# Layer 1 of a two-layer diffusion block: which heads are asked for one tile and which for all four at the start of the expert stage

## The chip, the cores and the metric

The kernel runs on one NeuronCore of a Trainium2 chip, in float32. The metric is the device time of one execution in microseconds (us): the median of three runs of the kernel before is 4263.29 us, with runs from 4258.36 to 4267.86 us.

## What is computed

Two consecutive layers of a diffusion backbone over 512 latent tokens and 256 context tokens of width 1024. Layer 0 mixes tokens with Fourier groups and a bidirectional state-space scan, layer 1 with latent attention. After each mixer comes the expert stage, which is all that matters here. It runs over blocks of 128 tokens, called tiles; layer 1 has four (the latent tokens only).

```python
def one(hb):                                   # one tile of 128 tokens
    q = (hb @ p["peer_wq"]).reshape(128, 8, 2, 128)
    s = jnp.einsum("thsd,hskd->thsk", q, p["peer_keys"])
    s_top, i_top = lax.top_k(s, 16)
    cand = (s_top[:, :, 0, :, None] + s_top[:, :, 1, None, :]).reshape(128, 8, 256)
    g_score, c_idx = lax.top_k(cand, 16)
    experts = e1 * 128 + e2                    # from i_top and c_idx
    gates = jax.nn.softmax(g_score, axis=-1)
    act = gelu(jnp.einsum("thkd,td->thk", peer_u[experts], hb)) * gates
    return jnp.einsum("thk,thkd->td", act, peer_v[experts])
```

For each token and each of 8 heads, two query halves are scored against 128 keys each, the best 16 of the 256 best sums are chosen, and the 16 experts' rows (1024 numbers of u and 1024 of v) are gathered from a table of 16384 experts.

## The kernel before, in words

`peer_block` (L1541) writes the expert stage of either layer; the table `PEER_MAPS` (L1502) holds what differs, and its second entry (L1520) is layer 1. Five engines run their own instruction streams and meet at semaphores; within a stream everything is in order.

**Asking.** An *event* is a head with the tiles it is asked for at once. Two query products, one for each half (`query`, L1974, its products on L1987), hold a 128x128 block of the head's query weights in the tensor engine (PE) and stream 128 columns for each tile of the event, over 8 blocks; then `scores` (L1991, products on L1998) multiplies by the keys, one product for each tile and half. ACT copies both out of the accumulation banks (`query_out` L2252, `scores_out` L2264). Before each event, SP loads its weights: two halves of 512 KB of the query weights (`load_side`, L1788) and 128 KB of keys (`load_keys`, L1792), one event ahead: the half of the next event is asked for when the product of this event's same half is done. Neighbouring events with the same head would share a load; `load_of` counts loads. Before, layer 1 has twelve events and twelve loads: heads 0 to 3 for tile 0, heads 4 to 7 for tiles 0 to 3, then heads 0 to 3 for tiles 1 to 3.

**Choosing.** The vector engine (DVE) picks the experts of one (head, tile), a *choice*, in two halves of work (`choose_a` L2524, `choose_b` L2555); a product on PE spreads it over the partitions (`spread_choice`, L1954, products on L1968), and `choice_out` (L2585, reading on L2590) writes the experts' numbers and gates. `order` lists the choices in the order in which they are made.

**Using.** A *step* is one (head, tile): 16 gathers of 1 MB each, one expert row for every token of the tile. Layer 1 has 32 steps in the order given by `heads`, four batches of four gathers each, 128 batches. POOL issues a gather (L1896) into one of 12 slots when its choice is written and the slot is free. DVE takes the dot products with the tokens (`dot_batch`, L2606, on L2614), ACT the gelu and the scaled diagonals (`diagonals`, L2432 and L2438), PE adds the weighted rows into two banks (L2186) and thereby frees the slots. The first 16 gathers use 8 slots; the other four are free once the attention's output product (`project`, L1914) is done.

**What sets the order.** All engines count batches. `half_at` (L1576) puts choice 2 into batches 3 and 4 and each later choice into the next two batches, so that the last of the 32 is made in batch 64. `query_at` (L1584 to L1588) then puts an event's first product five batches ahead of its first choice, at least two batches after the event before; its second product and first scores come one batch later, its second scores two. So before, events 4 to 11 start at batches 2, 6, 10, 14, 18, 24, 30 and 36. Events 0 to 3 and choices 0 and 1 are written out by hand in the opening, between the output products of the attention. In a batch, PE does the products of that batch first, then what is due of choices, spreads and events. `kept` names the events whose scores keep a buffer of their own; the others use two in turn. In batches 4 and 5, 36 and 37, and 68 and 69, PE also spreads the rows of the next tile (`spread_rows`, L1940).

The lines of SP's program that fix a load's place:

```python
sp.wait_ge(qmm["sem"], at(qmm, 2 * e - 1))
load_side(e, 0)
if e >= 2:
    sp.wait_ge(smm["sem"], at(smm, 2 * loads[n - 1]))
    load_keys(e)
sp.wait_ge(qmm["sem"], at(qmm, 2 * e))
load_side(e, 1)
```

Of the kernel before, what the change touches and what calls it, by code (L numbers as in the profile page):

```python
# [40 lines left out]
PH, PK, PQ, TOPK = 8, 128, 256, 16  # L41
# [1325 lines left out]
def attention_stage(core, d):  # L1367
# [30 lines left out]
    with nc.Block() as block:  # L1398
# [75 lines left out]
        def _(act):  # L1474
            for n in range(N + 2):
# [25 lines left out]
ALL = tuple(range(PH))  # L1501
# [15 lines left out]
     "rep": (L0 + 3072, L0 + 5120), "ht": HO,  # L1517
     "slots": [L0 + 7168 + n * ROWS for n in range(4)] + [RO + n * ROWS for n in range(6)] +
              [L0, L0 + 7168 + 4 * ROWS]},
    {"events": [(h, (0,)) for h in range(4)] + [(h, (0, 1, 2, 3)) for h in range(4, PH)] +  # L1520
               [(h, (1, 2, 3)) for h in range(4)],
     "heads": (ALL,) + (ALL[4:] + ALL[:4],) * 3, "kept": (4, 5, 6, 7),
     "order": [(h, 0) for h in range(4)] + [(h, t) for h in range(4, PH) for t in range(2)] +
              [(h, t) for h in range(4) for t in range(1, 4)] + [(h, t) for t in range(2, 4) for h in range(4, PH)],
     "choose_from": 3, "early": 2, "ahead": 4, "asked_from": 0, "spread_at": (4, 5), "spread_first": (4, 5),
     "halves": tuple((t, c) for t in range(TL) for c in range(2)),
     "opening": tuple(range(8)) * 2, "ready": 8, "column": (), "near": 2, "halved": (),
# [1386 lines left out]
ALL = ("ada0", "mix0", "mix1", "peer1")  # L2914
# [82 lines left out]
```

## Time and profile before

| | |
|---|---|
| median of three runs | 4263.29 us (4258.36 to 4267.86) |
| the profiled execution's own time | 4261.36 us |
| its span, first to last instruction | 4259.6 us |
| mean granted TensorE clock | 0.853 of full speed |
| PE busy | 3048.2 us (72%) |
| DVE busy | 2863.2 us (67%) |
| ACT busy | 1195.6 us (28%) |
| POOL busy | 1564.9 us (37%) |
| moved from memory | 1473.31 MB, of which 1342.26 MB by gathers |

The two expert stages take the larger part of the span: layer 0 has 768 gathers, layer 1 has 512, the first of them issued at 2921.8 us and the last at 4232.6 us. A line of the page gives an engine's busy time and its share of the span; a tenths line cuts the span into 40 slices of 106.5 us, each digit the busy share; the transfer line is the mean over the core's 16 DMA engines, and under it stand the GB/s that they moved. A line of the timeline starts with the start and the length in us (several instructions in a row are merged, and their number stands at the end), and in brackets stands how long the engine had been idle before it and what ended that. Large products of float32 appear as two records each.

### The profile page before, as it was taken

The numbers are of one execution on the slowest core, as the hardware profiler recorded it, in microseconds if no ns is written. First come the engines' busy times: TensorE is split into PE (matmuls) and PEld (weight loads), VectorE is DVE, ScalarE is ACT, GpSimd is POOL, SyncE is SP. The second block draws the span as 40 slices with busy tenths as digits, with TensorE's granted clock in tenths as the row PEclk, the third lists the DMA queues.
The fourth block names the chain that finished last, engine by engine and source line by source line (L and its number), as shares of the span: only waits on it lengthen the run. The fifth ranks groups of instructions, "written<-read, shape, count | busy, mean of one in ns | idle before, by whom it ended". The sixth has DMA issues, their size and how long they took to land. (4 is left out here: it accounts for less than half of the span.)

```text
span 4259.6 us, 37648 instructions
## 1 busy us (share of the span) xinstructions
PE 3048.2 (72%) x11946; PEld 1284.5 (30%) x11946; DVE 2863.2 (67%) x7196; ACT 1195.6 (28%) x3222; POOL 1564.9 (37%) x1352
## 2 busy tenths in 40 slices
PE   8999899766767755555666677998876654555556
PEld 4655444322222212111222223664322211111111
DVE  2436846998888897555555665665888898555555
ACT  2125423323223222111222353563332322111111
POOL 0002213454544454444444441002444555444443
PEclk9999999888788877777788888999987877777777
DMA  4114859999999999999999997106999999999998
GB/s 178 41 39 180 301 200 360 408 421 416 421 420 393 421 421 418 422 422 414 420 418 419 417 416 272 40 1 248 412 420 420 419 421 414 421 421 418 419 421 357
DMA packets 234010, 1481.23 MB, mean 348 GB/s; under 512 B 26060, under 2 KB 37548, under 8 KB 63572
## 3 DMA queue, kind: packets, MB, share of 16 engines
q0 software_dynamic: 184320, 1342.26, 76.2%
q1 hardware_dynamic: 48116, 132.61, 8.5%
q10 hardware_dynamic: 1376, 3.96, 0.2%
q8 instruction: 95, 1.56, 0.1%
q14 instruction: 103, 0.84, 0.1%
HBM read 1473.31 MB, written 5.42 MB: 347 GB/s over the span
## 5 line engine op out<-in xcount | busy, mean ns | idle before, releaser
L2186 PE MATMUL banks<-arena 128*64 128x512 f32 x5104 | 1636.3, 801 | 1152.8 <-ACT arena L2438 1094.9
L1896 POOL DMA_INDIRECT arena<-experts,arena x1280 | 1505.0, 1176 | 2221.3 <-PE banks L2186 1542.7
L2614 DVE CUSTOM_DVE_ANT_0 arena<-arena 128x1024 f32<-128x1024 f32 x1280 | 1538.9, 1223 | 841.5 <-DMA arena<-experts,arena 841.0
L2186 PEld LDWEIGHTS banks<-arena 128*64 128x64 f32 x5104 | 450.3, 182 | 2256.8 <-ACT arena L2438 1268.3
L2432 ACT ACTIVATE arena<-arena 128x4 f32<-128x4 f32 x319 | 65.9, 206 | 2267.7 <-DVE arena L2614 2267.6
L2438 ACT ACTIVATE arena<-arena 128x64 f32<-128x64 f32 x1276 | 339.3, 336 | 37.7 <-ACT arena L2432 1.2
L1987 PE MATMUL banks<-arena 128*128 128x512 f32 (+3 forms) x960 | 288.9, 455 | 6.7 <-DMA arena<-wq 5.6
L453 PE MATMUL banks<-arena 128*128 128x512 f32 (+1 forms) x640 | 210.3, 489 | 1.9 <-ACT arena L514 1.9
L1987 PEld LDWEIGHTS banks<-arena 128*128 128x128 f32 x960 | 160.5, 191 | 115.6 <-issue 90.2
L1914 PE MATMUL banks<-arena 128*128 128x512 f32 x416 | 187.9, 601 | 7.3 <-DMA arena<-l_w_out 3.1
L453 PEld LDWEIGHTS banks<-arena 128*128 128x128 f32 x640 | 121.3, 191 | 87.2 <-issue 78.6
L2432 ACT ACT_TABLE_LOAD x109 | 139.8, 1283 | 1.9
L942 POOL TENSOR_TENSOR arena<-arena 128x192 f32<-128x192 f32 x1 | 0.6, 579 | 305.1 <-POOLq L398 305.1
L2602 DVE TENSOR_TENSOR arena<-arena 128x512 f32<-128x512 f32 x160 | 109.7, 686 | 0.2 <-DVE arena L2592 0.2
L1914 PEld LDWEIGHTS banks<-arena 128*128 128x128 f32 x416 | 77.0, 191 | 97.6 <-issue 90.2
L2614 DVE DVE_READ_ACCUMULATOR2_ANT arena<- 128x1 f32 x1280 | 104.0, 81 | 0.0
L2279 ACT ACT_TABLE_LOAD x80 | 102.6, 1283 | 1.4
L1448 DVE TENSOR_REDUCE arena<-banks 128x1 f32<-128x768 f32 x64 | 61.1, 955 | 57.8 <-PE banks L1411 56.4
L1411 PE MATMUL banks<-arena 96*128 96x512 f32 (+1 forms) x256 | 94.7, 493 | 2.4 <-PEq L1785 1.5
L474 PE MATMUL banks<-arena 128*128 128x512 f32 x192 | 83.2, 593 | 0.0
L1482 ACT ACTIVATE arena<-banks 128x768 f32<-128x768 f32 x64 | 51.9, 810 | 67.9 <-PE banks L1420 67.9
L582 DVE TENSOR_SCALAR arena<-arena 128x772 f32<-128x772 f32 x16 | 10.9, 681 | 87.9 <-ACT arena L524 87.9
(269 smaller groups left out, 3039.0 us busy)
## 6 DMA issues: line engine op xcount, KB each, us to landing
arena<-l_w_ada SPq DMA_DIRECT2D x48, 1024.0 KB, 8.3
arena<-wq SPq DMA_DIRECT2D x54, 512.0 KB, 8.0
arena<-experts,arena POOLq DMA_INDIRECT x1280, 17.5
arena<-l_w_in SPq DMA_DIRECT2D x6, 2048.0 KB, 7.8
arena<-l_w_out SPq DMA_DIRECT2D x4, 1536.0 KB, 14.4
arena<-l_w_o SPq DMA_DIRECT2D x4, 1024.0 KB, 8.4
arena<-keys SPq DMA_DIRECT2D x27, 128.0 KB, 10.8
arena<-gates SPq DMA_DIRECT2D x6, 512.0 KB, 12.2
```

The source lines that it names most:

```text
L453: i = pe.matmul(o[:, a:b], wt[:, k, (u % 4) * P:(u % 4 + 1) * P], ht[:, k, a:b], start=(k == 0), stop=(k == KD - 1))
L474: i = pe.matmul(core["ps"][:, n % 4, :], ht[:, k, t * P:(t + 1) * P], wt[:, k, :], start=(k == 0), stop=(k == KD - 1))
L1411: i = pe.matmul(o[:, a:b], qt[0:QK, h, q * P:(q + 1) * P], kt[0:QK, h, a:b], start=True, stop=True)
L1896: pool.indirect_dma_start(slots[n], None, tbl, bass.IndirectOffsetOnAxis(ap=expert[:, ring[c], k:k + 1], axis=0)).then_inc(land[n]["sem"], ...
L1914: i = pe.matmul(core["ps"][:, bank_of(t, c), :], lhs(k, t), wcols[c][:, k, :], start=(k == 0), stop=(k == K - 1))
L1987: i = pe.matmul(out, wq[:, side, k, :], ht[:, g[0]:g[-1] + 1, k, :], start=(k == 0), stop=(k == KD - 1))
L2186: mm = pe.matmul(core["ps"][QS * j:QS * j + QS, c, :], diag[:, g % 2, k, :], v[:, D + c * 512:D + (c + 1) * 512], start=(g % (NB * PH) == ...
L2279: act.activation(raised, shifted, ACT.Exp, accum_out=total[:, 0:1]).then_inc(exd["sem"], up(exd))
L2432: act.activation(gel[:, s], dots[:, s], ACT.Gelu).then_inc(gl["sem"], up(gl))
L2438: ins = act.activation(diag[:, g % 2, j, :], gated[:, b // 2, b % 2 * BATCH + j, :], ACT.Copy, scale=gel[:, b * BATCH + j:b * BATCH + j + 1])
L2602: dve.tensor_tensor(gated[:, n % 2], ident2.unsqueeze(1).to_broadcast([P, TOPK // 2, QS]), bcast(gate[:, ring[c], n % 2 * 8:n % 2 * 8 + 8] ...
L2614: dve.tensor_tensor_reduce(u, u, rep[i // PH % 2][:, k % NQ, :], 1.0, 0.0, ALU.mult, ALU.add, dots[:, k:k + 1]).then_inc(dot["sem"], up(dot))
```

## The change

Only layer 1's entry of `PEER_MAPS` is edited. Heads 0 to 6 are asked for tile 0 alone, head 7 for all four tiles, and heads 0 to 6 follow for tiles 1 to 3. That makes fifteen events and fifteen loads. Only head 7's event keeps a buffer of its own. The steps of tiles 1 to 3 begin with head 7, and the choices are made in an order to match. The planner then starts events 4 to 14 at batches 2, 4, 6, 8, 12, 18, 24, 30, 36, 42 and 48.

```diff
-    {"events": [(h, (0,)) for h in range(4)] + [(h, (0, 1, 2, 3)) for h in range(4, PH)] +
-               [(h, (1, 2, 3)) for h in range(4)],
-     "heads": (ALL,) + (ALL[4:] + ALL[:4],) * 3, "kept": (4, 5, 6, 7),
-     "order": [(h, 0) for h in range(4)] + [(h, t) for h in range(4, PH) for t in range(2)] +
-              [(h, t) for h in range(4) for t in range(1, 4)] + [(h, t) for t in range(2, 4) for h in range(4, PH)],
+    {"events": [(h, (0,)) for h in range(7)] + [(7, (0, 1, 2, 3))] + [(h, (1, 2, 3)) for h in range(7)],
+     "heads": (ALL,) + (ALL[7:] + ALL[:7],) * 3, "kept": (7,),
+     "order": [(h, 0) for h in range(PH)] + [(7, 1)] + [(h, t) for h in range(7) for t in range(1, 4)] +
+              [(7, t) for t in range(2, 4)],
```

## Rows read from the trace of the kernel before

**Rows 1.** The page, busy time of each engine, and transfers over 40 slices.
```profile
PE 3048.2 (72%) x11946; PEld 1284.5 (30%) x11946; DVE 2863.2 (67%) x7196; ACT 1195.6 (28%) x3222; POOL 1564.9 (37%) x1352
...
DMA  4114859999999999999999997106999999999998
GB/s 178 41 39 180 301 200 360 408 421 416 421 420 393 421 421 418 422 422 414 420 418 419 417 416 272 40 1 248 412 420 420 419 421 414 421 421 418 419 421 357
```

**Rows 2.** Windows of layer 1's expert stage; columns are in the first line.
```profile
core 0: us, PE busy (x) PEld busy (x) DVE busy (x) ACT busy (x) POOL busy (x), PEclk, DMA share, GB/s
...
2970.00:2980.00 10.00, 8.55 (x60) 5.86 (x56) 5.89 (x14) 5.29 (x12) 7.86 (x8) 1.00 0.93 340
2980.00:2995.00 15.00, 9.73 (x22) 4.03 (x24) 13.48 (x45) 3.58 (x10) 0.81 (x1) 0.77 1.01 417
2995.00:3015.00 20.00, 20.00 (x115) 9.56 (x113) 11.36 (x39) 7.68 (x17) 7.85 (x9) 1.00 0.99 381
3015.00:3300.00 285.00, 211.12 (x830) 85.98 (x828) 250.53 (x741) 86.75 (x215) 138.85 (x108) 0.84 1.01 420
...
3360.00:3380.00 20.00, 12.00 (x59) 4.95 (x59) 18.32 (x55) 7.20 (x17) 10.50 (x9) 0.85 1.00 405
...
3520.00:3600.00 80.00, 42.22 (x160) 12.98 (x160) 72.03 (x215) 20.78 (x53) 40.92 (x32) 0.78 1.00 411
3600.00:4200.00 600.00, 341.07 (x1030) 95.60 (x1032) 320.08 (x525) 80.87 (x306) 256.33 (x237) 0.75 1.01 420
```

**Rows 3.** Waits of DVE, 2980 to 3060, then 3060 to 3600: total, times, longest.
```profile
DVE arena L2590 <- PE banks L1968: 6.7, 2, 6.0
...
DVE arena L2614 <- DMA arena<-experts,arena: 16.7, 17, 2.1
```

**Rows 4.** Transfers, 3050 to 3300: rate, queues, issues with median landing.
```profile
DMA packets 15776, 104.95 MB, mean 420 GB/s; under 512 B 1746, under 2 KB 2386, under 8 KB 3718
...
q0 software_dynamic: 13551, 98.68, 95.0%
q1 hardware_dynamic: 2212, 6.11, 6.3%
...
arena<-wq SPq DMA_DIRECT2D x10, 512.0 KB, 8.0
arena<-experts,arena POOLq DMA_INDIRECT x95, 17.4
arena<-keys SPq DMA_DIRECT2D x5, 128.0 KB, 10.7
```

**Rows 5.** Transfers, 3700 to 3900.
```profile
DMA packets 11559, 84.18 MB, mean 421 GB/s; under 512 B 1287, under 2 KB 1287, under 8 KB 1287
...
arena<-experts,arena POOLq DMA_INDIRECT x81, 17.5
```

**Rows 6.** Timeline of PE around batches 3 and 4, and one three-tile query side.
```profile
2975.02 3.74 PE L1987 MATMUL banks<-arena 128*128 128x128 f32 x32
...
2985.27 8.55 PE L1987 MATMUL banks<-arena 128*128 128x512 f32 x16 [5.60 <-DMA arena<-wq]
2993.75 3.65 PE L2186 MATMUL banks<-arena 128*64 128x512 f32 x16
...
2998.33 7.03 PE L1987 MATMUL banks<-arena 128*128 128x512 f32 x16
3005.29 3.65 PE L2186 MATMUL banks<-arena 128*64 128x512 f32 x16
...
3215.14 5.43 PE L1987 MATMUL banks<-arena 128*128 128x384 f32 x16
```

**Rows 7.** Timeline of POOL: first gathers of batches 6 and 7.
```profile
2995.95 0.94 POOL L1896 DMA_INDIRECT arena<-experts,arena  x1 [15.14 <-PE banks L2186]
...
3007.49 0.94 POOL L1896 DMA_INDIRECT arena<-experts,arena  x1 [6.88 <-PE banks L2186]
```

**Rows 8.** Line 1789, the query weights, 2900 to 3320.
```profile
DMA to landing us min/median/max: 3.3/8.0/13.8
```

## Prediction

> **What bounds the kernel now.** I read the profile from coarse to fine. First the whole span [rows 1]: no engine is busy for three quarters of it, but the transfer line shows 9 in nearly every slice of the two expert stages, at 414 to 421 GB/s. Then the stretch that the change touches, layer 1's expert stage from about 2920 us to the end, cut by windows [rows 2]. The reader should look at the last two columns: from 2970 us to 4200 us the transfer engines are busy at 0.99 or more of their time, but for 0.93 in the first 10 us, and in the long windows they move 420 GB/s whether the tensor engine is busy 0.75 of the time (3015 to 3300) or 0.57 (3600 to 4200). So the bytes set the end of this stage, and the 512 gathers are nearly all of them. Only four rows stay below 415 GB/s: 340 in 2970 to 2980, 381 in 2995 to 3015, 405 in 3360 to 3380 and 411 in 3520 to 3600. Against 420 those are 10 x 80/420 = 1.9 us, 20 x 39/420 = 1.9 us, 20 x 15/420 = 0.7 us and 80 x 9/420 = 1.7 us of transfer time not used. That is all that any rearrangement can win in there, 6.2 us. Third, the vector engine, which stands close behind: it is busy 0.88 of 3015 to 3300 and 0.90 of 3520 to 3600 [rows 2], and in all of 3060 to 3600 it waited only 16.7 us for a gather to land [rows 3]. So there are two limits near each other in the first half of the stage, and the transfers are the nearer.
>
> **The change, part by part.**
>
> *Three more weight loads.* An event loads two 512 KB halves of the query weights and 128 KB of keys: 1152 KB, 1.18 MB. Twelve events become fifteen, so 3.54 MB more, nine more transfers on SP's queue. The price per byte comes from two stretches. In 3050 to 3300 five events' loads pass beside 95 gathers [rows 4]; in 3700 to 3900 there is no load and there are 81 gathers [rows 5]. The total rate is 420 against 421 GB/s, so a load does not ride free, it takes the place of gathers. By the rate, 3.54 MB / 0.420 = 8.4 us. By what the loads' own queue used, 6.3% of 250 us for 6.11 MB is 2.58 us per MB, or 9.1 us. I take 8.7 us, between the two ends. All three new transfers' groups fall between batch 2 and batch 43, inside the stretch that runs at 420, so nothing covers them. The Trainium skill, DMA: Bandwidth & Descriptors, section Anatomy of one DMA, gives another price: a fixed 2.0 us for each transfer beside bytes / 436 GB/s. Paid one after the other that would be an estimate of 9 x 2.0 + 8.1 = 26 us; the trace does not agree, since ten half loads and five key loads passed in [rows 4] with no drop of the rate.
>
> *Shorter queries in the opening.* Heads 4, 5 and 6 are asked at batches 2, 4 and 6 (before: 2, 6, 10) and for one tile; head 7 at 8 for four tiles; heads 0 to 6 follow at 12, 18, 24, 30, 36, 42, 48 for three (before: four such at 18 to 36). A query side takes 3.74 / 2 = 1.9 us at one tile, 5.4 at three, 7.0 at four, and 8.55 us for the first one of head 4 [rows 6]. Where it hurts now: that first one waits 5.6 us for its weights, starts at 2985.27, and batch 3's products stand behind it until 2993.75, then the second side holds batch 4's until 3005.29 [rows 6]. POOL's next gathers wait 15.1 and 6.9 us for exactly those products [rows 7], and the rate falls to 381 [rows 2]. After the change the same weights land at the same time, so the 5.6 us stay; the side then takes 1.9 us at full clock, up to 3.7 us at half of it. Batch 3 starts 8.55 - 3.7 = 4.9 to 6.6 us sooner, and batch 4, with 7.0 - 1.9 = 5.1 us more, 10 to 11.7 us sooner. That is more than the shortfall of 1.9 us, so I take all of it back: -1.9 us. The bounds are 0 (a new wait) and -3.8 us (the hole at 2970 to 2980 too). I leave that hole in, because it ends before the first changed query starts. The vector engine gains as well: its 6.0 us wait for the tensor engine's spread of choice 2 [rows 3] should go, which lets it lie behind the transfers instead of beside them.
>
> *The end of the choosing.* The choices keep their rate, one in two batches until batch 64, so their vector time is the same. The shortfall of 3520 to 3600 comes after the last loads (batch 31 before, batch 43 after), when the vector engine no longer keeps ahead of the gathers. With more bytes and a vector engine that is 6 us further on, it should shrink; between 0 and -1.7 us, I take -0.9. The shortfall at 3360 to 3380 stays: a three-tile query still meets the spread of tile 2's rows at batch 36.
>
> *At nothing.* The tensor engine's sum: 8 x 1.9 + 8 x 7.0 + 8 x 5.4 = 114 us of query sides before, 14 x 1.9 + 2 x 7.0 + 14 x 5.4 = 116 us after. Its 2 us lie in stretches where it is busy three quarters of the time; without that cover they would cost 2 us. Twelve more evictions on ACT, which is busy 0.30 of 3015 to 3300 [rows 2], stand behind work of the same batch. The keys' wait on SP has only loads behind it; the store of tile 0 now stands ahead of head 5's loads, and goes out when the tile is done, at batch 32, as before. Scores are made per tile, 64 products before and after. The choice for step 16 is now out in batch 61, at the last allowed place, but the gathers it feeds wait for batch 61's products anyhow, and those follow the dots after which it is written.
>
> **Sum.** 8.7 - 1.9 - 0.9 = +5.9 us. The profiled execution took 4261.4 us (its span of 4259.6 and 1.8 around it), 1.9 us under the median of 4263.3; it would become 4267.3, and the median 4269.2 us, +0.14%. About 0.2% (8.5 us) is what a measurement of this kernel can tell from no change, so this is called the same.
>
> **The rivals.**
>
> *Slower: the loads at full price and nothing back.* The new loads of heads 5, 6 and 7 come two batches apart, some 20 us, and crowd the transfers just where they were short of gathers; a query that waits for its weights, as the first one of head 4 does for 5.6 us [rows 6], holds a batch's products and then the gathers. It decides if a weight load takes longer to land than the two batches it is given. Then the price is 9.1 us, plus up to two holes of 1.9 us like those of now: 4272.4 to 4276.2 us. For it: the loads are asked in order on one queue, each only after the query before it. Against it: landing took 8.0 us in the median and 13.8 at most [rows 8], under 20. Part of this case is that only the shortfall is misjudged: at 8.7 us alone the median is 4272.0, just beyond 0.2%.
>
> *Faster or level: the vector engine is the real limit of the first half.* Then loads cost nothing while gathers wait for dots, and the waits of 6.0 us and 0.7 us for the tensor engine [rows 3] come straight off: 4263.3 - 6.7 = 4256.6 us. For it: only 16.7 us of waiting for gathers in 540 us [rows 3]. Against it: the transfers have no such 6.7 us to give; they ran at 1.01 of their time through 3015 to 3300 [rows 2], and 3.54 MB more must pass.
>
> *A fixed price per transfer.* If each transfer held the engines for a time of its own beside its bytes, nine more would cost more than 3.54 MB. The fastest half load landed 3.3 us after its issue [rows 8], and its 0.52 MB at 420 GB/s are 1.25 us of that; the other 2.05 us, nine times, and 8.4 us for the bytes make 26.9 us, or 4290.2 us. Against it: fifteen loads passed in [rows 4] with the rate of [rows 5]. The page's formula above is this case.
>
> That the edit does less than it says (a load saved where two neighbouring events share a head) is out: no two neighbours in the new list do.
>
> **How the numbers follow.** The sum 0.63; slower 0.27; the vector engine as limit 0.07; a fixed price 0.03. The range goes from 4261 (the sum with its low bounds, 8.4 - 3.8 - 1.7 = +2.9 or 4266.2, and 5 us below it, as the runs shown lie up to 5 us from their median) to 4277 (the slower rival's upper end). Slower by over 0.2%: most of the slower rival, the fixed price and a small upper part of the sum, 0.29. Faster by over 0.2%: half of the vector engine's case, 0.04. The rest, 0.67, lies within.
>
> **What would show it.** Right: 30 half loads and 15 key loads in the stage in place of 24 and 12; the rate in the 20 us after head 4's first query near 420; POOL's 15.1 us wait cut by 5 us or more; the vector engine's wait for gathers over the choosing half above 16.7 us, as the transfers are now plainly the limit; the stretch from there to batch 64 longer by 6 to 7 us, and nothing different after. Wrong: a rate below 400 GB/s in the opening, DMA as the releaser of several queries, or gathers released by the vector engine's choices. If the rate stays at 420 and the end comes no later, the loads were hidden, and the first reading of the bound was false.

## The result, and the profile after

The changed kernel takes 4266.6 us (median of 18 runs) and the kernel before, in 18 runs beside them, 4259.4 us. The ratio is 1.0017 with a 95% interval of 1.0010 to 1.0023: 7.2 us longer, between 4 and 10 us. Forecast were +5.9 us and a time within 0.2%. The medians of before lie 4 us lower here than in the three runs that the prediction had, so the ratio counts, not the absolute time.

The profiled execution after has a span of 4266.2 us against 4259.6, 6.6 us more; the readings below are of this one. Behind the table every line number is one lower than before, because the table is one line shorter.

First the transfers of the stage, 2900 to 4270: queues, then issues with their size and median landing.

```profile
q0 software_dynamic: 73728, 536.90, 94.6%
q1 hardware_dynamic: 6624, 18.48, 3.5%
...
arena<-wq SPq DMA_DIRECT2D x28, 512.0 KB, 8.1
...
arena<-keys SPq DMA_DIRECT2D x13, 128.0 KB, 11.4
```

With the two groups loaded before 2900 that makes 30 half loads and 15 key loads. The gathers' bytes did not change; SP's queue moved 18.48 MB where it had moved 14.94, which is 3.54 MB more.

Now the windows of [rows 2], after; the last two columns are the share of time in which the transfer engines were busy and the GB/s.

```profile
2970.00:2980.00 10.00, 8.36 (x59) 5.72 (x54) 5.90 (x13) 5.48 (x13) 7.87 (x8) 1.00 0.93 358
2980.00:2995.00 15.00, 9.56 (x52) 6.72 (x54) 13.47 (x45) 5.75 (x17) 3.86 (x4) 0.77 1.00 403
2995.00:3015.00 20.00, 15.63 (x142) 10.25 (x140) 18.20 (x54) 5.74 (x16) 9.78 (x9) 0.94 1.02 416
3015.00:3300.00 285.00, 197.74 (x776) 80.80 (x772) 242.48 (x721) 83.03 (x213) 134.66 (x104) 0.85 1.01 420
...
3360.00:3380.00 20.00, 13.81 (x58) 5.57 (x56) 15.81 (x49) 6.02 (x13) 10.12 (x10) 0.86 1.02 419
...
3520.00:3600.00 80.00, 41.49 (x160) 12.63 (x158) 72.03 (x216) 21.66 (x56) 41.01 (x32) 0.78 1.01 412
3600.00:4200.00 600.00, 343.26 (x1024) 95.88 (x1020) 323.41 (x536) 79.81 (x302) 261.40 (x240) 0.74 1.01 420
```

The hole of 381 GB/s at 2995 to 3015 is filled to 416; the one at 2970 to 2980 stays, 358 for 340; in 2980 to 2995 the rate is lower than it was, 403 for 417. The one at 3360 to 3380 is gone from that window, and the low rate at 3520 to 3600 is still there, 412 for 411. In the two long windows the rate is what it was, with more to carry.

The tensor engine (PE) around batches 3, 4 and 5 after, from the timeline, to be held against [rows 6]:

```profile
2985.44 3.58 PE L1986 MATMUL banks<-arena 128*128 128x128 f32 x16 [5.97 <-DMA arena<-wq]
2988.95 3.65 PE L2185 MATMUL banks<-arena 128*64 128x512 f32 x16
...
2992.85 1.95 PE L1986 MATMUL banks<-arena 128*128 128x128 f32 x16
2994.73 3.65 PE L2185 MATMUL banks<-arena 128*64 128x512 f32 x16
```

And POOL's first gathers of batches 6 and 7, against [rows 7]:

```profile
2991.15 1.36 POOL L1895 DMA_INDIRECT arena<-experts,arena  x1 [10.53 <-PE banks L2185]
...
2996.94 1.02 POOL L1895 DMA_INDIRECT arena<-experts,arena  x1 [0.69 <-PE banks L2185]
```

Head 4's first side still waits for its weights (5.97 us for 5.60), then takes 3.58 us, nearly twice the 1.95 us of its second side: the tensor engine had stood idle ahead of it, and its granted clock was 0.50 from 2982 to 2988, the lower of its two levels (1.2 of 2.4 GHz), before and after alike. Batch 3's products start 4.8 us sooner and batch 4's 10.6 us sooner, and the gathers of batches 6 and 7 go out 4.8 and 10.6 us sooner. Following the first gather of each batch further shows where that lead goes: batch 8 is 9.4 us ahead, batch 12 is 0.2 us behind, batch 24 1.3, batch 40 1.1, batch 48 7.3, batch 64 7.0 and batch 127 6.9 us behind. The lead of ten microseconds is gone within five batches: gathers asked for sooner stand longer in the queue. Those issued from 2990 to 3055 land 20.2 us after their issue in the median, where they took 10.8 before. The transfers had been short of work for less than 2 us there. From there the new loads add up until the last of them; from batch 48 on the lag stays between 5.8 and 7.8 us.

The vector engine's (DVE) waits after, 2980 to 3060 and then 3060 to 3600: total, times, longest.

```profile
DVE arena L2613 <- DMA arena<-experts,arena: 6.7, 6, 1.3
...
DVE arena L2613 <- DMA arena<-experts,arena: 26.6, 25, 2.2
```

Its wait of 6.0 us for the tensor engine [rows 3] is gone, and in its place it waits for gathers, 26.6 us for 16.7 in the choosing half. It has got ahead, and stands behind the transfers.

### The profile page after: what moved, and what is told of

Read it like the earlier page. It is cut to its first block and busy times, and to the rows that moved or that the text cites. A ratio compares the mean times of both kernels' runs of the same rounds, so it can differ in the third digit from the quotient of the medians.

```text
span 4266.2 us, 37897 instructions
## 1 busy us (share of the span) xinstructions
PE 3062.4 (72%) x12042; PEld 1299.2 (30%) x12042; DVE 2863.2 (67%) x7196; ACT 1195.6 (28%) x3234; POOL 1556.5 (36%) x1352
## 5 line engine op out<-in xcount | busy, mean ns | idle before, releaser
L1986 PE MATMUL banks<-arena 128*128 128x128 f32 (+3 forms) x1056 | 290.5, 430 | 7.1 <-DMA arena<-wq 6.0
L1986 PEld LDWEIGHTS banks<-arena 128*128 128x128 f32 x1056 | 172.7, 193 | 106.1 <-issue 69.3
L453 PEld LDWEIGHTS banks<-arena 128*128 128x128 f32 x640 | 121.1, 191 | 87.4 <-issue 78.2
L1913 PEld LDWEIGHTS banks<-arena 128*128 128x128 f32 x416 | 77.6, 193 | 98.6 <-issue 91.3
## 6 DMA issues: line engine op xcount, KB each, us to landing
arena<-l_w_out SPq DMA_DIRECT2D x4, 1536.0 KB, 14.4
```

Source lines behind the costliest of these rows:

```text
L453: i = pe.matmul(o[:, a:b], wt[:, k, (u % 4) * P:(u % 4 + 1) * P], ht[:, k, a:b], start=(k == 0), stop=(k == KD - 1))
L1913: i = pe.matmul(core["ps"][:, bank_of(t, c), :], lhs(k, t), wcols[c][:, k, :], start=(k == 0), stop=(k == K - 1))
L1986: i = pe.matmul(out, wq[:, side, k, :], ht[:, g[0]:g[-1] + 1, k, :], start=(k == 0), stop=(k == KD - 1))
```

## The experiments

Ratios are to the kernel before, run beside each on the same chip, with the 95% interval. Three theories stood: *bytes* (the forecast: each load takes the place of gathers at 420 GB/s, the short queries give back a hole of 2 us), *the vector engine* as the limit of the first half, and *a fixed price* for each transfer.

**Loads alone.** The last three events of the kernel before load their query weights three times (`copies` is 3 for them and 1 for the others).

```diff
+                for n in range(copies(e)):
+                    if n:
+                        sp.wait_ge(wql[side]["sem"], wql[side]["total"])
-                sp.dma_start(wq[:, side], wq_d[:, 2 * events[e][0] + side]
-                             ).then_inc(wql[side]["sem"], up(wql[side], 16))
+                    sp.dma_start(wq[:, side], wq_d[:, 2 * events[e][0] + side]
+                                 ).then_inc(wql[side]["sem"], up(wql[side], 16))
...
```

What is left out of the cut counts the copies and lets each query wait for the last of its own.

> The kernel before, in which the query weights of its last three events (heads 1, 2 and 3 for tiles 1 to 3) are loaded three times in place of once, one copy after the other, the query waiting for the last: twelve half loads or 6.29 MB more, nothing else changed, the opening untouched. If bytes set the price (theory of the forecast): 6.29 MB / 0.420 = 15.0 us to 6.29 x 2.58 = 16.2 us longer than before, +0.35 to +0.38%, at an unchanged rate of 420 GB/s. If the vector engine is the limit of the first half: within 3 us of before. If each transfer has a fixed price of 2.05 us beside its bytes: 12 x 2.05 + 15.0 = 39.6 us, +0.93%.

Measured: 1.0036, 1.0023 to 1.0050, or 15.3 us (10 to 21) for 6.29 MB, 2.4 us per MB. The transfer view of 3150 to 3320, first the two queues of the kernel before, then queues and issues of this one:

```profile
q0 software_dynamic: 9244, 67.31, 95.2%
q1 hardware_dynamic: 1440, 4.06, 6.1%
```

```profile
q0 software_dynamic: 8589, 62.53, 88.5%
q1 hardware_dynamic: 2694, 8.66, 12.9%
...
arena<-wq SPq DMA_DIRECT2D x16, 512.0 KB, 8.0
```

Sixteen half loads in 170 us, each landing in 8.0 us as before, at 419 GB/s in all (420 in the same 170 us of the kernel before): SP's queue takes 12.9% of the engines' time where it took 6.1, and the gathers have 88.5 where they had 95.2. No query waits for a copy; the only wait for weights in the stage is the one of head 4's first side, 6.0 us. Bytes are paid in full. The fixed price, 39.6 us, is out, and so is a vector engine that would hide the loads and leave 3 us at most.

**The opening alone.** The changed kernel without its last three loads; heads 4, 5 and 6 for tiles 1 to 3 use head 3's weights and keys.

```diff
+    if layer == 1:
+        load_of = [min(n, 11) for n in load_of]
```

> The changed kernel without its last three loads: heads 4, 5 and 6 for tiles 1 to 3 are queried with the weights and keys of head 3 that are still there, so their choices are those of other weights; as many gathers, queries and choices as in the changed kernel, as many loads as before. This is the change's opening alone. Theory of the forecast (bytes; the shortfall at 2995 to 3015 is given back, the one at the end of the choosing is not): 0.7 to 0.85 MB sooner, so 1.7 to 2.0 us faster than before, about -0.04%, and 8.4 to 9.1 us faster than the changed kernel. If the opening gives nothing back and the loads are only cheaper than I took them: the same as before within 0.5 us, and 7.2 us faster than the changed kernel. If the vector engine is the limit: 6 to 7 us faster than before.

Measured: 0.9998, 0.9989 to 1.0007. Beside the 1.0017 of the change that is 0.19% or 8.1 us for three loads (3 to 13 us by the two intervals), which agrees with 8.4. The opening's gain is too small for this interval: -1 us, -4.7 to +3. The windows show it. They stand here for the whole opening, 2960 to 3015, of the kernel before, the changed kernel and this one:

```profile
2960.00:3015.00 55.00, 47.47 (x229) 24.00 (x231) 38.64 (x111) 19.68 (x48) 17.01 (x17) 0.94 0.99 388
2960.00:3015.00 55.00, 42.74 (x286) 27.20 (x287) 45.66 (x127) 20.02 (x54) 22.18 (x20) 0.92 1.00 400
2960.00:3015.00 55.00, 42.99 (x273) 26.17 (x273) 45.85 (x126) 21.56 (x55) 22.91 (x20) 0.89 1.00 400
```

400 for 388 GB/s over 55 us is 0.66 MB or 1.6 us. Each line is one execution, but the difference comes again: 387 in the kernel with tripled loads, which has the opening of before, and 398 in a kernel below with the opening of the change (lighter vector work). The vector engine's case, 6 to 7 us faster, is outside the interval.

**The hole made larger.** In the kernel before, head 4's two four-tile query sides are multiplied twice over. No byte more.

```diff
-                for k in range(KD):
+                for k in list(range(KD)) * (2 if layer == 1 and e == 4 else 1):
```

> The kernel before with both query sides of head 4 (four tiles, batches 2 and 3) multiplied twice over, the second pass starting the sums anew: 7 us more on the tensor engine ahead of batch 3's products and 7 us more ahead of batch 4's, no byte more, correct output. If the length of these two sides is what empties the transfers in the opening: the gathers of batch 6 go out 7 us later and those of batch 7 14 us later, the queue stands empty for most of that, and the kernel is 7 to 14 us longer than before (+0.16 to +0.33%), with a rate far below 381 GB/s between 2995 and 3030. If the hole comes from the wait of 5.6 us for the weights or from the slots alone: the same as before within 2 us.

Measured: 1.0034, 1.0022 to 1.0046, or 14.4 us (9 to 20). The two sides in the timeline, and then the windows:

```profile
2982.91 16.01 PE L1987 MATMUL banks<-arena 128*128 128x512 f32 x32 [5.37 <-DMA arena<-wq]
...
3003.43 13.90 PE L1987 MATMUL banks<-arena 128*128 128x512 f32 x32
```

```profile
2980.00:2995.00 15.00, 12.09 (x24) 5.38 (x25) 11.36 (x39) 0.55 (x3) 0.00 (x0) 0.77 0.89 356
2995.00:3015.00 20.00, 20.00 (x61) 8.61 (x60) 5.79 (x12) 3.94 (x10) 3.74 (x4) 1.00 0.65 243
3015.00:3030.00 15.00, 14.31 (x118) 7.71 (x116) 8.61 (x34) 4.77 (x9) 6.52 (x7) 1.00 0.70 253
```

The sides are 7.5 and 6.9 us longer than [rows 6], 14.3 us together, and the kernel is 14.4 us longer. The transfers' share falls to 0.65. So the length of these two products does make the hole, and past the point where the queue is empty each microsecond of them costs one. On the other side of that point it costs nothing: the change took 10.6 us out of the same place and only the 1.6 us that had been a hole came back.

**The same relief without a load.** Neighbouring events with one head share a load. Head 4 is asked for tile 0 and, two batches later, for tiles 1 to 3.

```diff
-    {"events": [(h, (0,)) for h in range(4)] + [(h, (0, 1, 2, 3)) for h in range(4, PH)] +
+    {"events": [(h, (0,)) for h in range(5)] + [(4, (1, 2, 3))] + [(h, (0, 1, 2, 3)) for h in range(5, PH)] +
                [(h, (1, 2, 3)) for h in range(4)],
...
```

The kept buffers and the order of the choices follow, with (4, 1), (4, 2) and (4, 3) taken early because that event now shares a buffer.

> The kernel before, in which head 4 is asked for tile 0 at batch 2 and, with the same loaded weights, for tiles 1 to 3 at batch 4 (neighbouring events with one head share a load: twelve loads as before); heads 5 to 7 for all tiles at 6, 10, 14 as before, and heads 0 to 3 four batches later, at 22, 28, 34, 40. Correct output. If the shortfall of 2995 to 3015 comes from the length of head 4's first two query sides: it goes, the rate there is above 410 GB/s, and the kernel is 1.0 to 1.9 us faster than before (-0.02 to -0.04%). If the long sides only have to come later (5.4 us a side at batches 4 and 5, beside 1.9 us of spreads each): the hole moves to 3015 to 3040 and the time is that of before within 0.5 us. If the vector engine is the limit: its 6.0 us wait goes and the kernel is up to 6 us faster.

Measured: 0.9993, 0.9984 to 1.0002. The forecast gain lies inside, and so does none; the time does not decide. The windows do, that of the hole and that of the whole opening:

```profile
2995.00:3015.00 20.00, 20.00 (x137) 11.59 (x138) 18.40 (x56) 7.50 (x20) 11.39 (x10) 1.00 1.02 421
2960.00:3015.00 55.00, 47.55 (x281) 28.83 (x282) 45.69 (x128) 21.66 (x58) 23.60 (x20) 0.94 1.00 407
```

The rate is 421, though the tensor engine is busy for all 20 us with the three-tile sides that now fall there. It is not how busy it is, but that no long product stands ahead of batches 3 and 4: their products start at 2988.90 and 2994.93, behind one-tile sides of 3.8 and 1.9 us. Over the opening 407 for 388 GB/s is 2.5 us, more than the change gets there, and head 4's first side still waits 5.5 us for its weights.

**One load less.** Head 3 is asked for tiles 1 to 3 right behind tile 0, with the weights that are there.

```diff
-    {"events": [(h, (0,)) for h in range(4)] + [(h, (0, 1, 2, 3)) for h in range(4, PH)] +
-               [(h, (1, 2, 3)) for h in range(4)],
-     "heads": (ALL,) + (ALL[4:] + ALL[:4],) * 3, "kept": (4, 5, 6, 7),
+    {"events": [(h, (0,)) for h in range(4)] + [(3, (1, 2, 3))] + [(h, (0, 1, 2, 3)) for h in range(4, PH)] +
+               [(h, (1, 2, 3)) for h in range(3)],
+     "heads": (ALL,) + (ALL[3:] + ALL[:3],) * 3, "kept": (5, 6, 7, 8),
+     "order": [(h, 0) for h in range(4)] + [(3, 1), (3, 2), (4, 0), (3, 3), (5, 0), (4, 1), (6, 0), (4, 2), (7, 0)] +
...
```

> A version that goes the other way: head 3 is asked for tile 0 and at once, with the same loaded weights, for tiles 1 to 3 (batch 2), heads 4 to 7 for all tiles at batches 6, 10, 14, 18, heads 0 to 2 for tiles 1 to 3 at 26, 32, 38: twelve events, eleven loads, 1.18 MB less than before and 4.72 MB less than the changed kernel. Correct output. Theory of the forecast (bytes): 2.8 to 3.0 us from the load and, the sides at batch 2 being 5.4 us and not 7 to 8.55 us, up to 1 us from the opening: 2.8 to 4.0 us faster than before, -0.07 to -0.09%. If the vector engine is the limit: the same as before within 1 us. If each transfer has a fixed price of 2.05 us: 2.8 + 6.2 = 9 us faster.

Measured: 0.9987, 0.9978 to 0.9996: 4255.8 us beside 4261.0, 5 us faster (2 to 9), the only one of these kernels that beats the one before beyond its interval. It is more than the 2.8 to 4.0 us that were expected, though those lie inside. Its timeline, and its window of the opening:

```profile
2976.90 5.33 PE L1988 MATMUL banks<-arena 128*128 128x384 f32 x16
2982.17 3.65 PE L2187 MATMUL banks<-arena 128*64 128x512 f32 x16
```

```profile
2960.00:3015.00 55.00, 46.16 (x253) 24.25 (x253) 47.04 (x131) 22.38 (x53) 25.71 (x21) 0.97 1.00 407
```

The query at batch 2 has no wait for weights in front of it, since they are head 3's: the 5.6 us of [rows 6] are gone too, and batch 3's products start at 2982.17. The opening gives 2.5 us (407 for 388 GB/s) where up to 1 us was expected, and with the 2.8 us of the load that makes 5.3. But the missing wait is not what makes the opening better: the kernel with head 4 split keeps that wait and has the same 407.

**The low rate at the end of the choosing.** Two kernels change the vector engine's work alone. The first is the changed kernel with half of two of its operations left out (half of each gated identity, half of each index product), so gates and experts are others.

```diff
+                w = TOPK if layer == 0 else TOPK // 2
-                dve.tensor_tensor(hot4, hot4, wheref.unsqueeze(2).to_broadcast([P, 2, TOPK, TOPK]),
+                dve.tensor_tensor(hot4[:, :, 0:w, :], hot4[:, :, 0:w, :], wheref.unsqueeze(2).to_broadcast([P, 2, w, TOPK]),
...
+                w = 8 if layer == 0 else 4
-                dve.tensor_tensor(gated[:, n % 2], ident2.unsqueeze(1).to_broadcast([P, TOPK // 2, QS]),
+                dve.tensor_tensor(gated[:, n % 2, 0:w], ident2.unsqueeze(1).to_broadcast([P, w, QS]),
...
```

> The changed kernel with less work on the vector engine in layer 1: each gated identity is written for 4 of its 8 slots and each index product for half of its rows, so gates and chosen experts are not the reference's; as many gathers, loads, queries and choices. About 0.34 us less in each choice and 0.34 us less for every two batches, some 0.34 us a batch while choices are made, 21 us in all. It settles the term of the forecast that failed, the rate of 411 to 412 GB/s at 3520 to 3600, which did not recover. If the vector engine makes it (it no longer keeps ahead of the gathers late in the choosing): the rate there rises to 418 or more and the kernel is 1.7 to 2.5 us faster than the changed kernel, so +0.11 to +0.13% against before. If the vector engine is the limit of the whole first half: about 20 us faster than the changed kernel, -0.3%. If something else makes the low rate: it stays at 411 to 413 and the time is that of the changed kernel, +0.17%.

Measured: 1.0009, 1.0000 to 1.0018, against 1.0017 for the change: 3.4 us less, and by the two intervals anything from 1 us longer to 8 us faster. The two operations take 0.42 and 0.43 us in place of 0.68 and 0.69, so 16 us of vector work are gone in 2960 to 3600 and not the 21 that were meant. The 20 us of a vector engine that limits the whole first half are out. The second is the kernel before with each gated identity of layer 1 written twice.

```diff
+                for again in range(layer + 1):
+                    if again:
+                        dve.wait_ge(gid["sem"], gid["total"])
                     dve.tensor_tensor(gated[:, n % 2], ident2.unsqueeze(1).to_broadcast([P, TOPK // 2, QS]),
...
```

What is left out of the cut makes ACT wait for the second writing.

> The kernel before with each gated identity of layer 1 written twice, one after the other: 0.68 us and the wait between the two more on the vector engine for every two batches, 0.34 to 0.4 us a batch, 22 to 25 us over the 62 batches with choices. Correct output. If bytes are the limit and the vector engine stands close behind (16.7 us of waiting for gathers in 3060 to 3600, and 8 us of waiting for other engines in the opening): the first 30 of these batches hide it behind the loads, the last 30, where the vector engine is hardly waiting, pay most of it: 6 to 10 us longer, +0.14 to +0.23%, with a rate below 410 GB/s in 3400 to 3600. If bytes were the plain limit: the same within 2 us. If the vector engine were the limit: 22 to 25 us longer, +0.5 to +0.6%.

Measured: 1.0000, 0.9991 to 1.0009. From 2960 to 3600 the trace has 60 of these writings, 0.69 us each, in place of 31: 20 us of further work on the engine that looked like the second limit cost nothing that can be measured. 6 to 10 us were expected of it if it stands close behind, and only a cost under 4 us lies inside the interval; of the cases on record, the plain limit of bytes is the one that fits.

What makes the low rate they don't show. The dips move from one execution to the next: 3520 to 3600 runs at 412 after the change, at 414 in the lighter kernel, but at 418 in the kernel without the reload, whose vector work is not lighter at all. The lighter kernel, the one without the reload and the heavier one:

```profile
3520.00:3600.00 80.00, 41.35 (x160) 12.71 (x160) 69.94 (x219) 21.66 (x56) 41.38 (x33) 0.79 1.01 414
3520.00:3600.00 80.00, 42.79 (x154) 12.81 (x152) 71.87 (x219) 21.66 (x56) 42.79 (x32) 0.79 1.01 418
3520.00:3600.00 80.00, 37.08 (x160) 11.70 (x156) 73.67 (x217) 20.39 (x51) 41.18 (x32) 0.83 1.00 409
```

So the whole stretch 3460 to 3680 is the fairer view, here before, after, without the reload, lighter and heavier:

```profile
3460.00:3680.00 220.00, 118.13 (x480) 37.75 (x478) 172.62 (x461) 50.25 (x138) 107.18 (x88) 0.79 1.01 417
3460.00:3680.00 220.00, 125.23 (x488) 42.62 (x486) 176.60 (x472) 53.20 (x147) 110.02 (x88) 0.79 1.01 417
3460.00:3680.00 220.00, 131.03 (x524) 45.37 (x522) 171.57 (x456) 51.50 (x144) 107.30 (x88) 0.82 1.01 418
3460.00:3680.00 220.00, 129.48 (x490) 43.86 (x492) 170.19 (x468) 53.47 (x147) 108.24 (x88) 0.78 1.01 418
3460.00:3680.00 220.00, 109.81 (x444) 34.61 (x442) 185.77 (x494) 51.75 (x143) 113.81 (x89) 0.81 1.00 411
```

Less vector work gives the 418 that the kernel without the reload has too. More vector work gives 411, but the heavier kernel's profiled execution took 4268.9 us, well above the median of 4262.6 of its runs, and was low in the opening already (367 GB/s from 2960 to 3015), so its windows are not its typical ones. That the vector engine has a part in the low rate is not shown; its cause stays open.

## Why the prediction was right, and where it was not

*The bound.* Right. The rate stayed at 420 GB/s and the bytes set the end; tripled loads cost 2.4 us per MB, and the vector engine could be given 20 us more while choices are made without a change of time beyond 4 us.

*Three more loads, 8.7 us.* Right: 3.54 MB at 420 GB/s are 8.4 us, and the change beside its own opening alone gives 8.1 us. Whether 8.4 or 9.1 us, the two ends that the 8.7 lies between, is nearer the runs cannot tell: the tripled loads fit 15.0 and 16.2 us alike. A fixed price of SP's transfers beside their bytes is at most 0.5 us by the tripled loads (21.3 us at the upper end less 15.0, over 12). The formula that the prediction quotes from the Trainium skill (DMA: Bandwidth & Descriptors, Anatomy of one DMA) is given there as a fit for transfers issued by GpSimd, a condition that the prediction left out; these loads go out on SP's queue.

*The opening, -1.9 us.* Right in place and size. Batch 3 came 4.8 us sooner (4.9 to 6.6 forecast, and the low clock after the wait made it the lower end), batch 4 10.6 us (10 to 11.7). Of the shortfall 1.6 us came back, from 4.2 us to 2.6 in 2960 to 3015; the times alone are too wide to show it. That the hole, not the products' time, bounds the gain is shown by the two kernels on either side: 10.6 us less gave 1.6 us in the windows, 14.3 us more cost 14.4 in the time.

*The end of the choosing, -0.9 us.* This term failed. "With more bytes and a vector engine that is 6 us further on, it should shrink": it did not. 411 became 412 at 3520 to 3600, the 40 us behind it fell from 422 to 413, and from 3460 to 3680 the rate is 417 before and after. The premise was that this low rate is the vector engine falling behind the gathers; nothing here shows that: the rate is 418 with lighter vector work and 418 with unchanged vector work and no reload, and the 411 with heavier work stands in an execution 6 us above its median. Measured, the term is nothing to within 0.5 us or so; why the rate is low there stays open.

*The shortfall at 3360 to 3380, to stay.* It left its window, 405 to 419, but nothing was won by that: 3340 to 3460 runs at the same rate before and after.

```profile
3340.00:3460.00 120.00, 78.40 (x346) 30.10 (x344) 108.93 (x328) 34.08 (x88) 63.28 (x48) 0.80 1.01 418
3340.00:3460.00 120.00, 88.71 (x388) 36.88 (x386) 103.02 (x313) 35.72 (x89) 55.38 (x45) 0.80 1.01 418
```

Between 3360 and 3380 the rate is 420 or 421 with the loads tripled, head 4 split, eleven loads, the lighter vector engine and the query twice, 408 without the reload and 385 with the heavier vector engine. What decides was not tried.

Together: 8.4 - 1.6 = 6.8 us, against 6.6 in the spans and 7.2 between the medians. So close an agreement is in part luck, for the interval goes from 4 to 10 us, and 1 GB/s more or less in the stretch of 220 us is already 0.5 us. By this sum the loads in the forecast of 5.9 were 0.3 us too dear and the opening 0.3 us too generous, which cancels; what is left of its error is the 0.9 us of the term that failed.

*The slower rival* was of the rivals the nearest in time. Its lower part, 8.7 to 9.1 us and nothing back from the opening, lies inside the interval, so the time does not rule it out; the opening's 400 for 388 GB/s does. Its mechanism did not come about: no query but head 4's first waits for weights, and the half loads land in 3.5 to 14.0 us after the change where they took 3.3 to 13.8 before [rows 8], still under the 20 us between two events. *The vector engine as limit* and *a fixed price per transfer* both fell, by the heavier vector engine and by the tripled loads.

*What was to be seen.* The counts, the rate in the opening (416), POOL's wait (4.6 us less, where 5 or more was said), the vector engine's longer wait for gathers, and 6 to 7 us by batch 64 with nothing after: all as written but for POOL's last half microsecond.

## What to carry to other kernels

Where transfers run at their full rate through a whole stage, price an edit by the bytes that it adds and by the holes in the rate that it can fill; the time that an engine gains ahead of such a queue is no gain beyond the hole. Before splitting a request to shorten the first part, look for a split that keeps the operand loaded: asking for the rest right behind the first part filled the hole here too, with no byte more, and with fewer it was 5 us faster. An engine that is 0.9 busy and hardly ever waits is not thereby the limit; give it more to do and see whether the end moves.

## What was not expected of the hardware

In the one profiled execution of the kernel with the second writing, the vector engine was busy for 0.92 of 3520 to 3600 (73.67 of 80 us) and waited for a gather only three times from 3060 to 3600, 3.8 us in all; yet the kernel's runs were as long as before within 0.09%. So an engine can look nearly without slack in a trace and still not show in the median time; that execution was itself 6 us above the median, and how much slack a run of median length has is not shown. And small loads on one queue beside 1 MB gathers on another took no more than their bytes, within the interval of 10 to 21 us for 15.0: sixteen half loads in 170 us landed in 8.0 us in the median, as ten in 250 us had [rows 4], at the same total rate.
